# The final norm of all tokens beside the last expert's block, whose own tokens are normed and stored over it

## The chip, the cores and the metric

The kernel runs on one core of a Trainium2 chip. The metric is device time in microseconds of one execution, as the median over several. Engines are named as in the profile: PE (TensorE), PEld (its weight loads), DVE (VectorE), ACT (ScalarE), POOL (GpSimd), SP (SyncE); a q behind a name means the sequencer of that engine.

## What is computed

A layer of a streaming encoder: a mixer (convolution and state space), then a mixture of experts over 2048 tokens of 1024 values, then a final RMS norm. Only the last two matter here.

```python
# top-1 of 4 groups, then top-2 of its 8 experts: 2 of 32 experts per token
h = rms_norm(x, g_ffn[l])
# per expert, in blocks of 128 tokens:
hid = jax.nn.silu(xblk @ w_gate[e]) * (xblk @ w_up[e])
yb = hid @ w_down[e]
x = x + segment_sum(yb * slot_gate, slot_token)      # each token gets two of these rows
return rms_norm(x, g_final)    # x * rsqrt(mean(x*x) + eps) * g_final
```

## The kernel before

`experts()` (L1773) is one block of code for all engines. Each expert has at least one block of 128 slots; the router's counts are known only at run time, so every engine loops in `over_blocks` (L1814): over the 32 experts, and in each over its `n` blocks. At the head of each expert an engine loads `n` and `start` from the tile `counts` into registers (L1817, L1818); ACT and DVE load a third number, `last` (L1819), which equals `n` except for the last expert, where it is never reached. In these inputs there are 46 blocks; the last expert has one.

A block `b`: PE computes gate and up halves (`hidden`), transposes the product (`turn_hidden`) and the next block's x (`turn_x`), and projects down (`down`, L2048). All products are made of float32 split in a high and a low part. DVE's `join` (L1956) makes `hid`, its `hid_low` (L1961) the low part `hl`, `turn_x` (L1950) that of x. ACT scales the result with the gate out of PSUM into `y` (L1906). POOL gathers the tokens of block b+2 (L1849), loads ids and gates (`ids_s`, L1873) as soon as the scatter of the block before has landed, and adds `y` to the rows of `residual` with an accumulating indirect DMA (L1879). Only one such scatter is under way at a time.

Weights: 6 pieces of 1 MB per expert (G0, U0, G1, U1, D0, D1). SP loads them to `raw` (L1629) when the piece before is split. In the last block of each expert but the last, ACT (`split_hi`, L1633) and DVE (`split_lo`, L1637) split those of the next expert between their other work; the test for it is `j == last - 1` (L1916, L2005). The order on DVE there: `join` 0, G0, U0, `hid_low` 0, `join` 1, `turn_x`, `hid_low` 1, G1, U1, D0, D1.

Behind this block of code stands a barrier of all engines (its drains carry line L1781), then `final_norm` (L2092), a block of its own. SP loads the 16 tiles of `residual` in five DMAs (L2109), ACT squares and sums each tile (L2122), DVE makes the scale of each group of tiles in 12 small steps (L2131, L61 to L71) and multiplies each tile by scale and gain (L2136); SP stores each tile when it is made (L2114). All 16 tiles have room in SBUF at once. The end is when all 16 stores have landed.

Of the kernel before, what the change touches and what calls it, by code (L numbers as in the profile page):

```python
# [6 lines left out]
FP32 = mybir.dt.float32  # L7
# [18 lines left out]
T8 = 8  # L26
# [118 lines left out]
def hybrid_encoder(nc, x, w_in, conv_b, log_dt, ssm_d,  # L145
# [21 lines left out]
    with ExitStack() as ctx:  # L167
# [19 lines left out]
        with ExitStack() as moe:  # L187
            weights = ExpertWeights(nc, moe, w_experts)
            experts(nc, scratch, ident, routing, weights)
        final_norm(nc, scratch, g_final, out)  # L190
# [1458 lines left out]
class Routing:  # L1649
# [6 lines left out]
    def __init__(self, nc, ctx):  # L1656
# [7 lines left out]
        self.counts, self.rows = sb("counts", [P, 3, NE], INT32), sb("rows", [1, P], INT32)  # L1664
# [108 lines left out]
def experts(nc, scratch, ident, routing, weights):  # L1773
# [7 lines left out]
    with ExitStack() as ctx:  # L1781
# [6 lines left out]
        y = sb("y", [P, D])  # L1788
        H = F // 2
# [33 lines left out]
        @block.sync  # L1823
        def _(sp):
# [5 lines left out]
            with sp.Fori(1, NE - 1) as e:  # L1830
                for u in range(weights.PIECES):
                    sp.wait_ge(w_lo, e * weights.PIECES + (u + 1))
                    weights.load(sp, e + 1, u)

        @block.gpsimd
        def _(pool):
# [30 lines left out]
            def body(b, e, j, last):  # L1867
# [8 lines left out]
                pool.wait_ge(ids_s_in, b * 16 + 16)  # L1876
                pool.wait_ge(y_done, b * 2 + 2)
# [5 lines left out]
            blocks = pool.value_load(counts[0:1, 1, NE - 1:NE], min_val=0, max_val=NBLK)  # L1883
            blocks = blocks + pool.value_load(counts[0:1, 0, NE - 1:NE], min_val=1, max_val=SEQ // P)
# [4 lines left out]
        def _(act):  # L1889
# [25 lines left out]
            def body(b, e, j, last):  # L1915
                with act.If(j == last - 1):  # L1916
# [24 lines left out]
            over_blocks(act, body, flags=True)  # L1941

        @block.vector
        def _(dve):
# [49 lines left out]
            step(V.tensor_scalar(n[:, NE - 1:NE], n[:, NE - 1:NE], float(2 * NBLK), None, ALU.add))  # L1994
            step(V.tensor_copy(counts[:, 2, :], n))
# [8 lines left out]
            def body(b, e, j, last):  # L2004
                with dve.If(j == last - 1):  # L2005
# [15 lines left out]
            over_blocks(dve, body, flags=True)  # L2021

        @block.tensor
        def _(pe):
# [44 lines left out]
            def body(b, e, j, last):  # L2069
# [9 lines left out]
                wait(pe, y_done, b * 2)  # L2079
# [7 lines left out]
                for i in range(2):  # L2087
                    down(b, 1, i).then_inc(down_done, 1)
            over_blocks(pe, body)


def final_norm(nc, scratch, g_final, out):  # L2092

    GROUPS = ((0, 2), (2, 6), (6, 10), (10, 14), (14, 16))
    with ExitStack() as ctx:  # L2095
        sb, _, sem = alloc(nc, ctx, "final")
        x = sb("x", [P, TT, D])
        gain, junk, st, scale = sb("gain", [P, D]), sb("junk", [P, D]), sb("st", [P, 4, TT]), sb("scale", [P, TT])
        gain_in, squared, own, made, stored = (sem(n) for n in ("gain_in", "squared", "own", "made", "stored"))
        x_in = [sem(f"x_in{g}") for g in range(len(GROUPS))]  # L2100
        block = ctx.enter_context(nc.Block())

        rows = scratch["acc"][0:SEQ, :].rearrange("(i p) d -> p i d", p=P)
        outs = out.rearrange("(h k s) d -> s h k d", s=T8, h=2)

        @block.sync
        def _(sp):
            for g, (first, end) in enumerate(GROUPS):
# [73 lines left out]
```

## Time and profile before

| | us |
|---|---|
| median of 3 runs | 1891.77 |
| lowest and highest run | 1879.50, 1892.37 |
| the profiled execution | 1895.12 |
| its span in the trace | 1893.7 |
| PE busy in the span | 1640.9 |
| DVE busy | 1116.7 |
| ACT busy | 803.3 |
| POOL busy | 605.9 |

Times of rows are microseconds from the start of the span. The profiled execution is 3.35 us longer than the median, and 1.4 us of it lie outside the span. PE's clock was granted at 0.924 of full speed over the span.

### The profile page before, as it was taken

How to read it: one execution, taken by the hardware profiler on the slowest of the kernel's cores; microseconds unless marked ns; L12 is line 12 of the kernel's file. 1: busy time of each engine (PE TensorE's matmuls, PEld its weight loads, DVE VectorE, ACT ScalarE, POOL GpSimd, SP SyncE). 2: the span in 40 equal slices, each digit the busy share in tenths (PEclk: the TensorE clock that was granted, in tenths of full speed). 3: DMA queues.
4: the chain of work that ended last, by engine and by line, in shares of the span. 5: the costliest groups of instructions: out<-in, count | busy, mean ns of one | idle time of the engine just before them, and what ended most of it. 6: DMA issues, size and time to landing. Idle time of an engine off the chain costs nothing. (4 is left out here: it accounts for less than half of the span.)

```text
span 1893.7 us, 33245 instructions
## 1 busy us (share of the span) xinstructions
PE 1640.9 (87%) x11171; PEld 1500.2 (79%) x11172; DVE 1116.7 (59%) x1707; ACT 803.3 (42%) x1022; POOL 605.9 (32%) x882
## 2 busy tenths in 40 slices
PE   7699999688937999999269999999999999999970
PEld 7599999577827888888268999899999888989860
DVE  7845564244547566665617646654666886665546
ACT  3222221012245333342315646644665775665543
POOL 0776774222323336444311212121222121212120
PEclk9899999878968898989579999999999999999995
DMA  8544342498854224312539878885877999887749
GB/s 278 169 146 147 127 161 85 121 223 247 225 200 137 97 89 134 101 67 90 215 119 316 275 240 272 274 285 188 291 273 257 382 366 359 280 275 254 261 137 366
DMA packets 166974, 403.90 MB, mean 213 GB/s; under 512 B 67967, under 2 KB 103169, under 8 KB 140417
## 3 DMA queue, kind: packets, MB, share of 16 engines
q1 hardware_dynamic: 140320, 336.26, 49.7%
q0 software_dynamic: 20080, 58.34, 12.7%
q10 hardware_dynamic: 6512, 8.51, 1.4%
q8 instruction: 36, 0.59, 0.1%
q14 instruction: 26, 0.21, 0.0%
HBM read 313.92 MB, written 89.13 MB: 213 GB/s over the span
## 5 line engine op out<-in xcount | busy, mean ns | idle before, releaser
L1637 DVE TENSOR_TENSOR expert_lo<-expert_raw,expert_hi 128x2048 fp32r<-128x2048 f32 x192 | 430.5, 2284 | 46.4 <-ACT expert_hi L1633 44.6
L1633 ACT CAST expert_hi<-expert_raw 128x2048 fp32r<-128x2048 f32 x192 | 361.6, 1910 | 18.1 <-DMA expert_raw<-in_experts 9.8
L720 PE MATMUL proj_p_z<-proj_x_hi,proj_w_hi 128*128 128x256 f32 x768 | 222.2, 289 | 14.1 <-DVE proj_x_lo L553 14.1
L721 PE MATMUL proj_p_z<-proj_x_lo,proj_w_hi 128*128 128x256 f32 x768 | 218.7, 285 | 0.0
L722 PE MATMUL proj_p_z<-proj_x_hi,proj_w_lo 128*128 128x256 f32 x768 | 218.5, 285 | 0.0
L2037 PE MATMUL moe_p_g0u<-expert_hi,moe_xh 128*128 128x256 f32 x736 | 210.8, 286 | 1.5 <-DVE moe_xl L1950 1.5
L2039 PE MATMUL moe_p_g0u<-expert_lo,moe_xh 128*128 128x256 f32 x736 | 206.6, 281 | 0.0
L2038 PE MATMUL moe_p_g0u<-expert_hi,moe_xl 128*128 128x256 f32 x736 | 206.6, 281 | 0.0
L2052 PE MATMUL moe_p_y<-expert_hi,moe_hh 128*128 128x512 f32 x368 | 153.4, 417 | 13.1 <-DVE moe_hl L1961 13.1
L1879 POOL DMA_INDIRECT residual<-moe_y,moe_ids_s x46 | 78.5, 1708 | 265.6 <-ACT moe_y L1906 258.1
L720 PEld LDWEIGHTS proj_p_z<-proj_x_hi,proj_w_hi 128*128 128x128 f32 x768 | 148.9, 194 | 14.2 <-issue 14.1
L721 PEld LDWEIGHTS proj_p_z<-proj_x_lo,proj_w_hi 128*128 128x128 f32 x768 | 149.0, 194 | 0.1
L722 PEld LDWEIGHTS proj_p_z<-proj_x_hi,proj_w_lo 128*128 128x128 f32 x768 | 148.7, 194 | 0.0
L2053 PE MATMUL moe_p_y<-expert_lo,moe_hh 128*128 128x512 f32 x368 | 145.2, 395 | 0.0
L2037 PEld LDWEIGHTS moe_p_g0u<-expert_hi,moe_xh 128*128 128x128 f32 x736 | 139.6, 190 | 4.0 <-issue 1.9
L2038 PEld LDWEIGHTS moe_p_g0u<-expert_hi,moe_xl 128*128 128x128 f32 x736 | 140.7, 191 | 2.0
L2039 PEld LDWEIGHTS moe_p_g0u<-expert_lo,moe_xh 128*128 128x128 f32 x736 | 139.7, 190 | 0.0
L1956 DVE TENSOR_TENSOR moe_hid<-moe_p_u,moe_sil 128x256 f32<-128x256 f32 x46 | 19.5, 424 | 172.6 <-PE moe_p_u L2039 135.9
L1873 POOL DMA_DIRECT2D moe_ids_s<-slot_table x46 | 25.8, 561 | 283.2 <-DMA residual<-moe_y,moe_ids_s 276.9
L2055 PE MATMUL moe_p_y<-expert_hi,moe_hl 128*128 128x512 f32 x368 | 115.8, 396 | 0.0
L1563 PE MATMUL mix_p_out<-mix_wo_hi,mix_cat_hi 128*128 128x512 f32 x256 | 107.4, 419 | 0.0
L1564 PE MATMUL mix_p_out<-mix_wo_hi,mix_cat_lo 128*128 128x512 f32 x256 | 105.8, 413 | 0.0
(416 smaller groups left out, 4149.9 us busy)
## 6 DMA issues: line engine op xcount, KB each, us to landing
expert_raw<-in_experts SPq DMA_DIRECT2D x192, 1024.0 KB, 6.2
ffn_input<-mix_h SPq DMA_DIRECT2D x17, 512.0 KB, 3.9
proj_x_sb<-in_x SPq DMA_DIRECT2D x8, 1024.0 KB, 7.3
mix_x_sb<-in_x SPq DMA_DIRECT2D x16, 512.0 KB, 5.0
residual<-mix_x SPq DMA_DIRECT2D x16, 512.0 KB, 2.7
out<-final_x SPq DMA_DIRECT2D x16, 512.0 KB, 6.4
proj_x_raw<-in_x_turned SPq DMA_DIRECT2D x7, 1024.0 KB, 4.8
proj_w_raw<-in_w_in SPq DMA_DIRECT2D x8, 768.0 KB, 7.3
```

What stands on the lines that cost most here:

```text
L720: nc.tensor.matmul(o, whi, x_hi[:, half, c], start=start, stop=False)
L721: nc.tensor.matmul(o, whi, x_lo[:, half, c], start=False, stop=False)
L722: return nc.tensor.matmul(o, wlo, x_hi[:, half, c], start=False, stop=stop)
L1563: nc.tensor.matmul(o[:, :], cat_hi[:, par, k, ts], wo_hi[:, k, sl], start=c == 0, stop=False)
L1633: self.nc.scalar.copy(self.hi[:, u], self.raw[:, u]).then_inc(self.hi_done, 1)
L1637: tensor_tensor(self.lo[:, u], self.raw[:, u], self.hi[:, u].bitcast(FP32), ALU.subtract).then_inc(self.lo_done, 1)
L2037: nc.tensor.matmul(out, xh[:, c], w_hi, start=c == 0, stop=False)
L2038: nc.tensor.matmul(out, xl[:, c], w_hi, start=False, stop=False)
L2039: last_mm = nc.tensor.matmul(out, xh[:, c], w_low, start=False, stop=c == KD - 1)
L2052: nc.tensor.matmul(p_y[i][:, :], hh[:, c], w_hi, start=c == 0, stop=False)
L2053: nc.tensor.matmul(p_y[i][:, :], hh[:, c], w_low, start=False, stop=False)
L2055: last_mm = nc.tensor.matmul(p_y[i][:, :], hl[:, c], weights.outer(hi, D0 + i, c), start=False, stop=c == F // P - 1)
```

## The change

The function `final_norm` goes, and with it the barrier ahead of it. `experts()` loops over 31 experts; the last one has code of its own on each engine. When all scatters ahead of the last expert have landed, POOL signals (`acc_complete`), and SP loads the 16 tiles of `residual` in pairs of 1 MB into the six pieces of `raw`, which are free by then. Pair 6 and pair 7 take the room of pairs 0 and 1, once these are stored. ACT squares all tiles (into `y`) and DVE norms them, in groups of 4, 6 and 6 tiles, behind their other work on the last expert's first block. The last expert does not scatter into `residual`: POOL gathers the rows of `residual` of the block's tokens into `r`, DVE adds PSUM times the gate to it, ACT squares it, DVE norms it, and POOL scatters the rows into `out` when all 16 tiles have been stored. `out` has 128 rows more, for the slots that hold no token, and its rows stand in the order of `residual`; the host puts them in order. `counts` loses its third row, and ACT and DVE the value load of `last`.

```diff
-            experts(nc, scratch, ident, routing, weights)
-        final_norm(nc, scratch, g_final, out)
+            experts(nc, scratch, ident, routing, weights, g_final, out)
...
-        self.counts, self.rows = sb("counts", [P, 3, NE], INT32), sb("rows", [1, P], INT32)
+        self.counts, self.rows = sb("counts", [P, 2, NE], INT32), sb("rows", [1, P], INT32)
...
+        gain, r = sb("gain", [P, D]), sb("r", [P, D])
+        fst, fscale, rst = sb("fst", [P, 3, TT]), sb("fscale", [P, TT]), sb("rst", [P, 6])
...
+        LAST = NE - 1
+        PAIRS = TT // 2
+        GROUPS = ((0, 2), (2, 5), (5, 8))
+        gain_in, acc_complete, stored = sem("gain_in"), sem("acc_complete"), sem("stored")
+        tiles_in = [sem(f"tiles_in{g}") for g in range(PAIRS)]
+        squared, norm_own, made = sem("squared"), sem("norm_own"), sem("made")
+        r_in, y_last, r_squared, r_own, r_done = (sem(n) for n in ("r_in", "y_last", "r_squared", "r_own", "r_done"))
...
-        def over_blocks(engine, body, before=None, flags=False):
-            with engine.Fori(0, NE) as e:
+        def tile_of(i):
+            return weights.raw[:, i // 2 % weights.PIECES, i % 2 * D:(i % 2 + 1) * D]
+        def last_blocks(engine):
+            n = engine.value_load(counts[0:1, 0, LAST:NE], min_val=1, max_val=SEQ // P)
+            return n, engine.value_load(counts[0:1, 1, LAST:NE], min_val=0, max_val=NBLK)
+        def over_blocks(engine, body):
+            with engine.Fori(0, LAST) as e:
                 n = engine.value_load(counts[0:1, 0, bass.ds(e, 1)], min_val=1, max_val=SEQ // P)
                 start = engine.value_load(counts[0:1, 1, bass.ds(e, 1)], min_val=0, max_val=NBLK)
-                last = engine.value_load(counts[0:1, 2, bass.ds(e, 1)], min_val=1, max_val=3 * NBLK) if flags else None
                 with engine.Fori(0, n) as j:
-                    body(start + j, e, j, last)
+                    body(start + j, e, j, n)
...
+            acc = scratch["acc"][0:SEQ, :].rearrange("(i p) d -> p i d", p=P)
+            outs = out[0:SEQ, :].rearrange("(i p) d -> i p d", p=P)
+            def load_tiles(g):
+                to = weights.raw[:, g % weights.PIECES].rearrange("p (i d) -> p i d", d=D)
+                sp.dma_start(to, acc[:, 2 * g:2 * g + 2]).then_inc(tiles_in[g], 16)
+            sp.dma_start(gain[:, :], g_final.partition_broadcast(P)).then_inc(gain_in, 16)
+            sp.wait_ge(acc_complete, 1)
+            for g in range(weights.PIECES):
+                sp.wait_ge(w_lo, LAST * weights.PIECES + (g + 1))
+                load_tiles(g)
+            for g in range(PAIRS):
+                for i in (2 * g, 2 * g + 1):
+                    sp.wait_ge(made, i + 1)
+                    sp.dma_start(outs[i], tile_of(i)).then_inc(stored, 16)
+                if g + weights.PIECES < PAIRS:
+                    sp.wait_ge(stored, 32 * (g + 1))
+                    load_tiles(g + weights.PIECES)
+            sp.wait_ge(stored, 16 * TT)
...
-            def body(b, e, j, last):
+            def fetch(b, e, j):
                 pool.wait_ge(x_in, b * 16 + 32)
                 pool.sem_inc(gathers, 1)
                 load_ids(row_of(b + 2))
...
                 pool.wait_ge(x_turned, b * 2 + 4)
                 gather(b + 2)
                 pool.wait_ge(ids_s_in, b * 16 + 16)
+            def body(b, e, j, n):
+                fetch(b, e, j)
                 pool.wait_ge(y_done, b * 2 + 2)
                 pool.sem_inc(scatters, 1)
                 nc.gpsimd.indirect_dma_start(out=scratch["acc"][:, :],
                                              out_offset=bass.IndirectOffsetOnAxis(ap=ids_s[:, 0:1], axis=0),
                                              in_=y[:, :], in_offset=None, compute_op=ALU.add).then_inc(scattered, 16)
             over_blocks(pool, body)
-            blocks = pool.value_load(counts[0:1, 1, NE - 1:NE], min_val=0, max_val=NBLK)
-            blocks = blocks + pool.value_load(counts[0:1, 0, NE - 1:NE], min_val=1, max_val=SEQ // P)
+            n, start = last_blocks(pool)
+            pool.wait_ge(scattered, start * 16 + 16)
+            pool.sem_inc(acc_complete, 1)
+            with pool.Fori(0, n) as j:
+                b = start + j
+                fetch(b, LAST, j)
+                pool.sem_inc(gathers, 1)
+                nc.gpsimd.indirect_dma_start(out=r[:, :], out_offset=None, in_=scratch["acc"][:, :],
+                                             in_offset=bass.IndirectOffsetOnAxis(ap=ids_s[:, 0:1], axis=0)).then_inc(r_in, 16)
+                pool.wait_ge(r_done, j + 1)
+                pool.wait_ge(stored, 16 * TT)
+                pool.sem_inc(scatters, 1)
+                nc.gpsimd.indirect_dma_start(out=out[:, :],
+                                             out_offset=bass.IndirectOffsetOnAxis(ap=ids_s[:, 0:1], axis=0),
+                                             in_=r[:, :], in_offset=None).then_inc(scattered, 16)
+            blocks = start + n
             pool.wait_ge(scattered, blocks * 16 + 16)
             pool.wait_ge(x_in, blocks * 16 + 32)
...
-            def body(b, e, j, last):
-                with act.If(j == last - 1):
+            def squares():
+                for i in range(TT):
+                    act.wait_ge(tiles_in[i // 2], 16)
+                    nc.scalar.activation(y[:, :], tile_of(i), ACT.Square, accum_out=fst[:, 0, i:i + 1]).then_inc(squared, 1)
+                    act.wait_ge(squared, i + 1)
+            def last_expert():
+                n, start = last_blocks(act)
+                with act.Fori(0, n) as j:
+                    b = start + j
+                    silu(b, 0)
+                    silu(b, 1)
+                    hid_high(b, 0)
+                    turn_x(b + 1)
+                    hid_high(b, 1)
+                    with act.If(j == 0):
+                        squares()
+                    for i in range(2):
+                        act.wait_ge(y_last, j * 2 + (i + 3))
+                        nc.scalar.activation(sil[:, :], r[:, i * 512:(i + 1) * 512], ACT.Square,
+                                             accum_out=rst[:, i:i + 1]).then_inc(r_squared, 1)
+                        act.wait_ge(r_squared, j * 2 + (i + 1))
+            def body(b, e, j, n):
+                with act.If(j == n - 1):
...
-            step(V.tensor_scalar(n[:, NE - 1:NE], n[:, NE - 1:NE], float(2 * NBLK), None, ALU.add))
-            step(V.tensor_copy(counts[:, 2, :], n))
...
-                with dve.If(j == last - 1):
+            def final_norm():
+                step = Chain(dve, norm_own)
+                dve.wait_ge(gain_in, 16)
+                for first, end in GROUPS:
+                    dve.wait_ge(squared, 2 * end)
+                    w = slice(2 * first, 2 * end)
+                    step(V.tensor_scalar(fst[:, 1, w], fst[:, 0, w], 0.5 / D, 0.5 * EPS, ALU.mult, ALU.add))
+                    rsqrt(nc, step, fscale[:, w], fst[:, 1, w], fst[:, 2, w])
+                    for i in range(2 * first, 2 * end):
+                        V.scalar_tensor_tensor(out=tile_of(i), in0=tile_of(i), scalar=fscale[:, i:i + 1],
+                                               in1=gain[:, :], op0=ALU.mult, op1=ALU.mult).then_inc(made, 1)
+            def last_expert():
+                n, start = last_blocks(dve)
+                dve.sem_inc(y_last, 2)
+                with dve.Fori(0, n) as j:
+                    b = start + j
+                    join(b, 0)
+                    hid_low(b, 0)
+                    join(b, 1)
+                    turn_x(b + 1)
+                    hid_low(b, 1)
+                    with dve.If(j == 0):
+                        final_norm()
+                    dve.wait_ge(ids_s_in, b * 16 + 16)
+                    dve.wait_ge(r_in, j * 16 + 16)
+                    for i in range(2):
+                        dve.wait_ge(down_done, b * 2 + (i + 1))
+                        half = slice(i * 512, (i + 1) * 512)
+                        V.scalar_tensor_tensor(out=r[:, half], in0=p_y[i][:, :], scalar=ids_s[:, 1:2].bitcast(FP32),
+                                               in1=r[:, half], op0=ALU.mult, op1=ALU.add).then_inc(y_last, 1)
+                    step = Chain(dve, r_own, j * (RSQRT_COLUMN_STEPS + 2))
+                    dve.wait_ge(r_squared, j * 2 + 2)
+                    step(V.tensor_tensor(rst[:, 2:3], rst[:, 0:1], rst[:, 1:2], ALU.add))
+                    step(V.tensor_scalar(rst[:, 3:4], rst[:, 2:3], 0.5 / D, 0.5 * EPS, ALU.mult, ALU.add))
+                    rsqrt_column(nc, step, rst[:, 4:5], rst[:, 3:4], rst[:, 5:6])
+                    assert step.n == RSQRT_COLUMN_STEPS + 2
+                    V.scalar_tensor_tensor(out=r[:, :], in0=r[:, :], scalar=rst[:, 4:5], in1=gain[:, :],
+                                           op0=ALU.mult, op1=ALU.mult).then_inc(r_done, 1)
+            def body(b, e, j, n):
+                with dve.If(j == n - 1):
...
-            over_blocks(dve, body, flags=True)
+            over_blocks(dve, body)
+            last_expert()
...
-            def body(b, e, j, last):
+            def block_of(b, e, room):
                 pe.wait_ge(x_lo, b * 2 + 2)
                 wait(pe, hid_done, b * 2)
...
-                wait(pe, y_done, b * 2)
+                room()
...
+            def body(b, e, j, n):
+                block_of(b, e, lambda: wait(pe, y_done, b * 2))
             over_blocks(pe, body)
...
-def final_norm(nc, scratch, g_final, out):
...
+            n, start = last_blocks(pe)
+            with pe.Fori(0, n) as j:
+                def room():
+                    wait(pe, y_done, start * 2)
+                    pe.wait_ge(y_last, j * 2 + 2)
+                block_of(start + j, LAST, room)
...
-    out = nc.dram_tensor("out", (1, SEQ, D), FP32, kind="ExternalOutput").ap()
+    out = nc.dram_tensor("out", (1, ROWS, D), FP32, kind="ExternalOutput").ap()
     hybrid_encoder(nc, *args, out[0])
     r = _run(nc, [arrays], core_ids=[0])
-    return r.results[0]["out"]
+    by_step = _np.asarray(r.results[0]["out"])[:, :SEQ].reshape(1, T8, 2, P, D)
```

## Rows read from the trace of the kernel before

**Rows 1.** Windows: stretch, its length, busy us (x instructions) of each engine, clock, DMA.
```profile
986.00:1836.00 850.00, 825.47 (x5942) 764.79 (x5940) 540.25 (x456) 510.81 (x547) 174.24 (x180) 1.00 0.82 278
...
1847.00:1894.00 47.00, 0.00 (x0) 0.00 (x0) 29.16 (x76) 18.38 (x32) 0.00 (x0) 0.50 0.93 368
...
1859.00:1871.00 12.00, 0.00 (x0) 0.00 (x0) 6.95 (x17) 9.87 (x17) 0.00 (x0) 0.50 1.03 411
```

**Rows 2.** The page's chain that ended last, by line, as shares of the span.
```profile
DVE final_x L2136 1%; DMA final_x<-residual 1%; ACT final_junk L2122 0%; DVE final_scale L71 0%; DVE final_st L70 0%; DVE final_st L69 0%; DVEq L2095 0%; DVE final_scale L62 0%; DVE final_scale L61 0%; SPq L2111 0%; DVE final_st L2131 0%; SPq L2109 0%; ACTq L2120 0%
```

**Rows 3.** Waits, 1000 to 1836: us in total, times, longest.
```profile
PEld moe_p_hid L2045 <- DVE moe_hid L1956: 15.9, 25, 1.1
...
PE moe_p_y L2052 <- DVE moe_hl L1961: 13.1, 18, 0.8
...
DVE moe_hid L1956 <- issue: 35.1, 30, 1.7
```

**Rows 4.** Timeline of DVE at an expert's begin: start, us, what [idle before].
```profile
1800.17 4.49 DVE L1637 TENSOR_TENSOR expert_lo<-expert_raw,expert_hi 128x2048 fp32r<-128x2048 f32 x2 [1.48 <-ACT expert_hi L1633]
1806.10 0.42 DVE L1956 TENSOR_TENSOR moe_hid<-moe_p_u,moe_sil 128x256 f32<-128x256 f32 x1 [1.44 <-issue]
```

**Rows 5.** DVE sequencer's value loads: whole run, then there: ns min/median/max, starts.
```profile
L1817 DVEq TENSOR_LOAD <-routing_counts x32: 302/844/1387, 964.7 to 1822.6; - x32
...
L1818 DVEq TENSOR_LOAD <-routing_counts x1: 303/303/303, 1804.4 to 1804.4; - x1
...
L1819 DVEq TENSOR_LOAD <-routing_counts x1: 302/302/302, 1805.1 to 1805.1; - x1
```

**Rows 6.** Timeline of ACT: the second half of `y`, last three blocks.
```profile
1797.65 0.69 ACT L1906 ACTIVATE moe_y<-moe_p_y,moe_ids_s 128x512 f32<-128x512 f32 x1 [0.65 <-PE moe_p_y L2055]
...
1817.51 0.69 ACT L1906 ACTIVATE moe_y<-moe_p_y,moe_ids_s 128x512 f32<-128x512 f32 x1 [0.65 <-PE moe_p_y L2055]
...
1835.54 0.69 ACT L1906 ACTIVATE moe_y<-moe_p_y,moe_ids_s 128x512 f32<-128x512 f32 x1 [0.65 <-PE moe_p_y L2055]
```

**Rows 7.** DMA, us to landing: weights; all of tile `final_x`; last scatter.
```profile
expert_raw<-in_experts SPq DMA_DIRECT2D x178, 1024.0 KB, 6.1
...
DMA to landing us min/median/max: 2.7/6.5/22.5
...
residual<-moe_y,moe_ids_s POOLq DMA_INDIRECT x1, 6.3
```

**Rows 8.** Timeline of DVE in the final norm: first small step, first multiplications.
```profile
1854.67 0.17 DVE L2131 TENSOR_SCALAR final_st<-final_st 128x2 f32<-128x2 f32 x1 [22.49 <-ACT final_junk L2122]
...
1857.04 2.48 DVE L2136 SCALAR_TENSOR_TENSOR final_x<-final_x,final_scale,final_gain 128x1024 f32<-128x1024 f32 x2
```

**Rows 9.** Timeline of POOL in the last block.
```profile
1829.63 0.56 POOL L1873 DMA_DIRECT2D moe_ids_s<-slot_table  x1 [5.17 <-DMA residual<-moe_y,moe_ids_s]
...
1837.04 1.66 POOL L1879 DMA_INDIRECT residual<-moe_y,moe_ids_s  x1 [5.45 <-ACT moe_y L1906]
```

**Rows 10.** Timelines of SP and ACT: first load, first and third tile squared.
```profile
1847.44 0.38 SPq L2109 DMA_DIRECT2D final_x<-residual  x1
...
1852.31 1.06 ACT L2122 ACTIVATE final_junk<-final_x 128x1024 f32<-128x1024 f32 x1 [16.08 <-DMA final_x<-residual]
...
1853.49 1.06 ACT L2122 ACTIVATE final_junk<-final_x 128x1024 f32<-128x1024 f32 x1
...
1859.44 1.06 ACT L2122 ACTIVATE final_junk<-final_x 128x1024 f32<-128x1024 f32 x1 [4.80 <-DMA final_x<-residual]
```

**Rows 11.** Timeline of DVE: two subtractions of 128x512 out of PSUM.
```profile
1829.90 1.29 DVE L1950 TENSOR_TENSOR moe_xl<-moe_p_x,moe_xh 128x512 fp32r<-128x512 f32 x2 [0.56 <-ACT moe_xh L1893]
```

**Rows 12.** POOL's drains at the ends of the expert and norm stages: ns, start.
```profile
L1781 POOLq DRAIN  x1: 3615/3615/3615, 1843.6 to 1843.6; - x1
...
L2095 POOLq DRAIN  x1: 46/46/46, 1847.4 to 1847.4; - x1
```

**Rows 13.** The page's DMA queues: the busier instruction queue, whole span.
```profile
q8 instruction: 36, 0.59, 0.1%
```

More of the change, by code:

```diff
@@ L1770, in gates, with experts @@
         step(E.tensor_tensor(pay[:, :, 1, 1].bitcast(FP32), recip, exps[:, :, NG], ALU.mult))
-def experts(nc, scratch, ident, routing, weights):
+def experts(nc, scratch, ident, routing, weights, g_final, out):
     hi, lo, w_lo = weights.hi, weights.lo, weights.lo_done
@@ L1940, in body @@
                         scale_y(b, i)
-            over_blocks(act, body, flags=True)
+            over_blocks(act, body)
+            last_expert()
         @block.vector
@@ L2020, in body @@
                     hid_low(b, 1)
-            over_blocks(dve, body, flags=True)
+            over_blocks(dve, body)
+            last_expert()
         @block.tensor
@@ L2067, in _ @@
             pe.wait_ge(routed, COUNTED)
-            def body(b, e, j, last):
+            def block_of(b, e, room):
                 pe.wait_ge(x_lo, b * 2 + 2)
@@ L2088, in body @@
                     down(b, 1, i).then_inc(down_done, 1)
+            def body(b, e, j, n):
+                block_of(b, e, lambda: wait(pe, y_done, b * 2))
             over_blocks(pe, body)
-def final_norm(nc, scratch, g_final, out):
[L2094 to L2108, printed above, removed]
-                sp.dma_start(x[:, first:end], rows[:, first:end]).then_inc(x_in[g], 16)
-                if g == 0:
-                    sp.dma_start(gain[:, :], g_final.partition_broadcast(P)).then_inc(gain_in, 16)
-            for i in range(TT):
-                sp.wait_ge(made, i + 1)
-                sp.dma_start(outs[i // 2][i % 2], x[:, i]).then_inc(stored, 16)
-            sp.wait_ge(stored, 16 * TT)
-        @block.scalar
-        def _(act):
-            for g, (first, end) in enumerate(GROUPS):
-                act.wait_ge(x_in[g], 16)
-                for i in range(first, end):
-                    nc.scalar.activation(junk[:, :], x[:, i], ACT.Square, accum_out=st[:, 0, i:i + 1]).then_inc(squared, 1)
-                    act.wait_ge(squared, i + 1)
-        @block.vector
-        def _(dve):
-            step = Chain(dve, own)
-            for g, (first, end) in enumerate(GROUPS):
-                dve.wait_ge(squared, end)
-                w = slice(first, end)
-                step(nc.vector.tensor_scalar(st[:, 1, w], st[:, 0, w], 0.5 / D, 0.5 * EPS, ALU.mult, ALU.add))
-                rsqrt(nc, step, scale[:, w], st[:, 1, w], st[:, 2, w])
-                if g == 0:
-                    dve.wait_ge(gain_in, 16)
-                for i in range(first, end):
-                    nc.vector.scalar_tensor_tensor(out=x[:, i], in0=x[:, i], scalar=scale[:, i:i + 1],
-                                                   in1=gain[:, :], op0=ALU.mult, op1=ALU.mult).then_inc(made, 1)
@@ L2177 @@
             for name, a in arrays.items()]
-    out = nc.dram_tensor("out", (1, SEQ, D), FP32, kind="ExternalOutput").ap()
+    out = nc.dram_tensor("out", (1, ROWS, D), FP32, kind="ExternalOutput").ap()
     hybrid_encoder(nc, *args, out[0])
     r = _run(nc, [arrays], core_ids=[0])
-    return r.results[0]["out"]
+    by_step = _np.asarray(r.results[0]["out"])[:, :SEQ].reshape(1, T8, 2, P, D)
+    return _np.ascontiguousarray(by_step.transpose(0, 2, 3, 1, 4)).reshape(1, SEQ, D)
```

## Prediction

> **What bounds the kernel now.** I read the windows first. The expert stage is 850 of the 1893.7 us of the profiled span and PE is busy in 825 of it; in the last 47 us PE is idle, with DVE busy 29 us and ACT 18, and the 11 us between the two hold only the last scatter and a barrier [rows 1]. The chain of waits that ended last runs through the final norm alone: DVE's multiplication first, then the load of the tiles, ACT's squares, DVE's small steps [rows 2]. So the change works on some 57 us, from the last block's scatter to the end. In steady work DMA is the second bound there: share 1.03 at 411 GB/s [rows 1], and the stage reads and writes 8.4 MB each, 41 us at that rate.
>
> Then I read the waits of the expert stage, because the diff also takes something out of a loop that runs 31 more times. PE hardly waits for anything but DVE: 25 waits of its weight loads for `hid` (15.9 us) and 18 for `hl` at the down projection [rows 3]. DVE, on its side, starts `hid` late with no partner named: 30 times "issue", 35.1 us [rows 3]. A timeline shows it: D0 and D1 of the next expert are split by 1804.66, `join` of the next block starts at 1806.10, 1.44 us later [rows 4]; the splits of G0 and U0 and `hid_low` come behind it. In that hole DVE's sequencer does its value loads one after the other: the second starts at 1804.4, the third at 1805.1 [rows 5]. Such an expert of one block takes 19.86 us (second half of `y` at 1797.65 to 1817.51); the block behind it, which has no splits to wait for, takes 18.03 (to 1835.54) [rows 6].
>
> **The change, part by part.**
>
> *One value load less at each expert, on DVE and ACT.* `last` (L1819) goes; the comparison takes `n`. On DVE its load is 0.30 us and the register work around it comes to about as much: start to start it is 0.7 us [rows 5]. I take 0.65, since the starts are rounded. ACT runs ahead in its queue there (no hole), so nothing for it. Where is 0.65 us on the path? In an expert of one block the path is closed: down projection, ACT scales `y`, splits D0, DVE splits D0 and D1, value loads, `join`, two more splits, `hid_low`, down projection. PE waits in it twice, so its own 18 us don't bind and the full 0.65 us comes off. PE's 18 waits for `hl` count these blocks: 18 x 0.65 = 11.7 us. The loads run 32 times [rows 5], the first before any block, so there are 31 boundaries; the other 13 have no splits behind `join`; PE gains only what it waited for `hid`. Of the 25 such waits at least 7 are theirs, mean 15.9 / 25 = 0.64: I take 4 us. Together 15.7 us. Lower bound 0 (if another wait is right behind in each), upper 31 x 0.7 = 21.7. DMA is the cover to look at: with shorter blocks the 6 weight loads of 1 MB per expert come closer together. They land 6.1 us after issue, a third of a block [rows 7], so I cost this at nothing; if that cover went, the gain would be lost where one-block experts stand side by side, at most the 11.7 us.
>
> *Two DVE steps for `counts[:, 2]`* go, once, 0.4 us by the 0.2 us of a small step [rows 8]; beside PE's transpose. Nothing.
>
> *The final norm begins when the scatter before the last has landed.* POOL now sees this with the id load at 1829.63 [rows 9]; it signals SP, whose first load I put at 1829.3 against 1847.44 [rows 10], 18.1 us sooner. Everything of the last block that PE does (to 1835) is covered by this, for DVE comes back to `p_y` only at 1877. The barrier (with POOL's drain of 3.6 us from 1843.6 [rows 12]) goes from between the stages, but see below.
> Loads: the first 1 MB was squared from 1852.31, 4.9 us after its issue; the next 2.5 MB took 7.1 us more [rows 10]. Pair 0 lands at 1834.2. Pairs follow every 2.6 us. POOL's two gathers (the unused one of x and that of `r`, 0.5 MB each, 2.5 us of DMA time) lie between, so pair 4 is in at 1847.1 and pair 5 at 1849.7. ACT needs 1.18 us per tile (1852.31 to 1853.49) [rows 10], keeps up, and has ten tiles squared at 1849.5. DVE's second group: 2.4 us of small steps (1854.67 to 1857.04), six multiplications at 1.2 [rows 8]: 1859.1.
> Now the ring of 6 pieces of `raw` holds 12 tiles. SP waits for tiles 0 and 1 to be stored; their stores lie behind pair 5 on the queue, 1.3 us each: 1852.3. Pair 6 lands at 1857.2; tiles 2 and 3 lie behind it, 1859.8; only then pair 7, landed 1864.7. Its squares are done at 1867.1, small steps 1869.5, six multiplications 1876.7. The stores of tiles 4 to 15 queue behind pair 7: 12 x 1.25 = 15 us, 1879.7.
> The old kernel has its last store landed at about 1893.3, 0.4 us ahead of its end, so the 18 us have become 14 already: two round trips of a store and a load eat the rest.
>
> *The last block's own tokens.* All on the path behind 1876.7: two additions of 128x512 out of PSUM, like those of `xl` (1.29 us for two) [rows 11]; a half tile's square 0.9 with its wait; ten column steps at 0.2, 2.0; a multiplication, 1.3: `r_done` at 1882.3. By then all tiles are stored. POOL starts 0.8 us later, as it does behind `y` (1835.54 and 0.69 against 1837.04) [rows 6, 9]: 1883.1. The scatter without addition is not in the trace: below, a store of as many bytes by SP takes 2.7 us at its shortest [rows 7] and POOL's instruction 1.66 [rows 9], 4.4; above, the accumulating scatter on a quiet chip, 6.3 [rows 7]. I take 5.2, as it has half the traffic of the latter: 1888.3.
>
> *The end.* In the old kernel SP sees its store land and all is over 0.4 us later: POOL, long idle, drains in 46 ns. Behind its own indirect DMAs the same POOL needs 3615 ns [rows 12]. POOL is now the last engine of the last block of code, so this drain moves to the very end: 0.3 + 3.6, 1892.2. Bounds 0.05 and 3.6; I take 3.6, the row of this same place.
> The tail gives 1893.7 - 1892.2 = 1.5 us.
>
> **Sum.** 15.7 + 1.5 = 17.2 us: span 1876.5. The profiled execution took 1895.12 with a median of 1891.77 over the runs; taken off the median, 1874.6, which I call **1875 us**.
>
> The Trainium skill, "DMA: Bandwidth & Descriptors" (section on the anatomy of one DMA on the software path), gives about 2.0 us plus bytes over 436 GB/s for a DMA. For 0.52 MB an estimate from that page is 3.2 us, half of what the quiet scatter's row shows; with it the sum would be 2 us better.
>
> **Rivals.**
> A. *The value load is hidden anyway*: DVE's join then waits for something else as long. For it: DVE's first load of the three takes from 302 to 1387 ns [rows 5], so something unseen stretches it. Against: the loads run one after the other and `join` follows the last. Time: 1891.8 - 1.5 = 1890.
> B. *The tail does worse*: pair 7 comes later, because a load or store under traffic takes 6.5 us in the median [rows 7] and not 1.3 behind a load. Two round trips 4 us longer: tail 8 us worse, 1883.
> C. *Both do better*: a drain of 0.1 us and a scatter of 4.4 make the tail 5.8 us, the loop gives 20: 1891.8 - 25.8 = 1866. For it: no row shows a drain long behind a plain scatter.
> D. *Slower*: code. The last expert has code of its own on every engine, and loops whose code moved may have to be fetched anew at each branch back. It decides from (18.9 + 17.2) / 31 = 1.2 us per expert on PE or DVE; at 1.3 us it gives 1915. Against it: the busier instruction queue carried 36 packets in the whole span [rows 13], against 46 blocks on four engines, so loop bodies stay in place. New straight code for one block falls under the 41 us of slack that PE has.
> Of this the Trainium skill says, in "Runtime: NRT & Kernel Launch", section on instruction fetch, that a taken branch whose target is outside the window of two pages stalls for a fetch. By the packet counts the trace doesn't show that happening in these loops.
>
> **How the numbers follow.** Forecast 0.56 (1868 to 1881, loop 12 to 19 and tail -1 to +5), A 0.17, B 0.10, C 0.11, D 0.06. A measurement of this kernel tells 1% from no change, which is 18.9 us: below 1872.9 is faster, above 1910.7 slower. Of the forecast's own range nearly half lies below 1872.9, with C and a little of the others: faster 0.38; slower D and a rest, 0.07; within 1%, 0.55. The range is 1864 to 1890: it takes in C, B and most of A, leaves out D and the far ends.
>
> **What would show it.** Right: one-block experts of 19.2 us in place of 19.86; DVE's idle "issue" before `hid` near 0.5 us in place of 1.2 (35.1 / 30); PE's waits for `hid` nearly gone; first tile load 18 us ahead of where the old one would be; a hole in ACT's squares before tiles 12 and 14; POOL's scatter last, then a long POOL drain. Wrong: one-block experts still at 19.9 (A), tile 14 squared more than 40 us after the first load (B), a POOL drain under 1 us (C), or holes on PE at each expert with nothing named (D).

## The result and the profile after

| | before | after |
|---|---|---|
| median, us | 1885.63 (4 runs, 1878.65 to 1892.37) | 1861.03 (4 runs, 1853.94 to 1867.52) |
| ratio | | 0.987, 95% interval 0.984 to 0.990 |
| span of the profiled execution, us | 1893.7 | 1865.5 |
| expert stage in the profile, us: from the second half of `y` of block 0 to that of block 44 | 831.07 | 811.18 |
| from there to the end of the span (the tail), us | 76.2 | 76.7 |

The change makes the kernel 1.3% faster. That is outside "within 1%", and 1861.03 is 3 us under the range. The last two rows are the finding in short. They split the span at the second half of `y` of the last block ahead of the last expert (1817.51 in [rows 6]). In the profile of after these are the rows of the timeline of ACT:

```profile
977.61 0.69 ACT L1961 ACTIVATE moe_y<-moe_p_y,moe_ids_s 128x512 f32<-128x512 f32 x1 [0.65 <-PE moe_p_y L2175]
...
1788.79 0.69 ACT L1961 ACTIVATE moe_y<-moe_p_y,moe_ids_s 128x512 f32<-128x512 f32 x1 [0.65 <-PE moe_p_y L2175]
```

The first in the profile of before is:

```profile
986.44 0.69 ACT L1906 ACTIVATE moe_y<-moe_p_y,moe_ids_s 128x512 f32<-128x512 f32 x1 [0.65 <-PE moe_p_y L2055]
```

So 19.9 us of the 28.1 between the two profiles lie in a stage from which the diff takes one value load per expert. 8.8 us lie ahead of block 0, where next to nothing was changed (and the profiled execution of before, 1895.12 us, was slower than all four of the table). In the eleven profiles of this case the stretch ahead of block 0 takes from 971.8 to 986.4 us, whatever the edit. And the stage that was rewritten got 0.6 us longer.

**The loop.** The waits of the expert stage after, in the columns of [rows 3] (us in total, times, longest), answer to those rows:

```profile
PEld moe_p_hid L2165 <- DVE moe_hid L2036: 2.2, 7, 0.4
...
PE moe_p_y L2172 <- DVE moe_hl L2041: 9.1, 16, 0.8
...
DVE moe_hid L2036 <- issue: 13.0, 21, 0.9
```

DVE's hole "issue" before `hid` went from 35.1 to 13.0 us, and PE's waits for `hid` from 15.9 to 2.2. At 9 of the 30 experts that begin between block 0 and block 44 the hole is gone (under 0.1 us), as in this timeline of DVE (start, us, what), to be read against [rows 4]: D0 and D1 are split by 1556.05 and `hid` follows at once. The next expert's `hid` comes 18.40 us later; for the same expert it was 19.10 before (1579.62 to 1598.72, the last two lines).

```profile
1551.56 4.49 DVE L1636 TENSOR_TENSOR expert_lo<-expert_raw,expert_hi 128x2048 fp32r<-128x2048 f32 x2 [1.49 <-ACT expert_hi L1632]
1555.97 0.42 DVE L2036 TENSOR_TENSOR moe_hid<-moe_p_u,moe_sil 128x256 f32<-128x256 f32 x1
...
1574.37 0.42 DVE L2036 TENSOR_TENSOR moe_hid<-moe_p_u,moe_sil 128x256 f32<-128x256 f32 x1
```
```profile
1579.62 0.42 DVE L1956 TENSOR_TENSOR moe_hid<-moe_p_u,moe_sil 128x256 f32<-128x256 f32 x1 [1.02 <-issue]
...
1598.72 0.42 DVE L1956 TENSOR_TENSOR moe_hid<-moe_p_u,moe_sil 128x256 f32<-128x256 f32 x1 [0.69 <-issue]
```

Where the loads lie explains the hole. Here are DVE's two value loads at the expert above, then at one where a hole was left (its last split ends at 1776.55, `hid` starts at 1777.40):

```profile
L1835 DVEq TENSOR_LOAD <-routing_counts x1: 347/347/347, 1554.1 to 1554.1; - x1
...
L1836 DVEq TENSOR_LOAD <-routing_counts x1: 324/324/324, 1554.8 to 1554.8; - x1
```
```profile
L1835 DVEq TENSOR_LOAD <-routing_counts x1: 1323/1323/1323, 1774.6 to 1774.6; - x1
...
L1836 DVEq TENSOR_LOAD <-routing_counts x1: 319/319/319, 1776.3 to 1776.3; - x1
```

At each of the 30 beginnings, in all eleven profiles, the first load starts 1.92 to 1.96 us ahead of the end of the last split, and where a hole is left `hid` starts 0.73 or 0.85 us behind the end of the last load (0.93 or 1.05 in e9, which has arithmetic there). So the first 1.1 to 1.2 us of the loads are hidden under the last split; only what goes beyond that is the hole. In the kernel before every hole was at least 0.67 us long, so the third load, 0.30 us and 0.41 us of register work behind the second, came off almost in full.

**The tail.** SP's timeline, then ACT's and DVE's (the part on the path), then POOL's last scatter and, from the view of one line, its drain:

```profile
1800.08 3.11 SPq L1857 DMA_DIRECT2D expert_raw<-residual  x6
1814.25 1.55 SPq L1867 DMA_DIRECT2D out<-expert_raw  x2
1823.78 0.38 SPq L1857 DMA_DIRECT2D expert_raw<-residual  x1
...
1832.95 0.38 SPq L1857 DMA_DIRECT2D expert_raw<-residual  x1
```
```profile
1830.52 1.06 ACT L1974 ACTIVATE moe_y<-expert_raw 128x1024 f32<-128x1024 f32 x1 [6.82 <-DMA expert_raw<-residual]
...
1839.23 1.06 ACT L1974 ACTIVATE moe_y<-expert_raw 128x1024 f32<-128x1024 f32 x1 [6.38 <-DMA expert_raw<-residual]
```
```profile
1841.59 0.17 DVE L2089 TENSOR_SCALAR moe_fst<-moe_fst 128x6 f32<-128x6 f32 x1 [10.76 <-ACT moe_y L1974]
...
1844.01 7.26 DVE L2092 SCALAR_TENSOR_TENSOR expert_raw<-expert_raw,moe_fscale,moe_gain 128x1024 f32<-128x1024 f32 x6
...
1855.82 1.28 DVE L2120 SCALAR_TENSOR_TENSOR moe_r<-moe_r,moe_rst,moe_gain 128x1024 f32<-128x1024 f32 x1
```
```profile
1858.00 0.98 POOL L1936 DMA_INDIRECT out<-moe_r,moe_ids_s  x1 [47.84 <-DVE moe_r L2120]
```
```profile
L1782 POOLq DRAIN  x1: 3697/3697/3697, 1861.6 to 1861.6; - x1
```

The first load starts 11.3 us behind the `y` of block 44; in the old kernel [rows 10] it was 29.9 us. The 18.6 us won there are spent again, in two places. From the first load to the end of the last multiplication the new kernel takes 51.2 us (1800.08 to 1851.27), the old one 43.1 (1847.44 to 1890.54, the end of the line below): ACT stands 6.8 us and then 6.4 us for pairs 6 and 7, whose loads SP may issue only at 1823.78 and 1832.95, when tiles 0 and 1, then 2 and 3, are stored; DVE stands 10.8 us. Behind the last tile come 6.7 us of the last block's own tokens, 3.3 us of scatter and 3.7 us of drain, 14.3 us with what lies between; the old kernel had its own tokens, its scatter and that drain ahead of its norm, and 3.1 us behind it. So 8.1 and 11.1 us more, 19.2 together.

```profile
1888.06 2.48 DVE L2136 SCALAR_TENSOR_TENSOR final_x<-final_x,final_scale,final_gain 128x1024 f32<-128x1024 f32 x2
```

### The profile page after: what moved, and what is told of

It reads as the page before. It is cut to its first block, busy times and chain, and to the rows that moved or that the text cites. A ratio compares the mean times of both kernels' runs of the same rounds, so it can differ in the third digit from the quotient of the medians.

```text
span 1865.5 us, 32975 instructions
## 1 busy us (share of the span) xinstructions
PE 1628.9 (87%) x11171; PEld 1493.3 (80%) x11172; DVE 1116.0 (60%) x1694; ACT 801.1 (43%) x1024; POOL 603.0 (32%) x883
## 4 chain that ended last, share of the span: by engine, by line
PE 33%; issue 6%; DMA 4%; DVE 3%; ACT 2%; DVEq 2%; POOL 1%; ACTq 0%; SPq 0%; POOLq 0%
PE moe_p_y L2172 5%; PE moe_p_y L2175 4%; PE moe_p_y L2173 4%; PE moe_p_g0u L2157 3%; PE moe_p_g0u L2159 3%; PE moe_p_g0u L2158 3%; DVE expert_lo L1636 2%; ACT expert_hi L1632 2%; PE moe_p_x L2149 1%; PE moe_p_g L2159 1%; PE moe_p_u L2159 1%; PE moe_p_g L2158 1%; PE moe_p_u L2157 1%; PE moe_p_u L2158 1%; PE moe_p_g L2157 1%
## 5 line engine op out<-in xcount | busy, mean ns | idle before, releaser
L1920 POOL DMA_INDIRECT residual<-moe_y,moe_ids_s x45 | 76.5, 1700 | 251.8 <-ACT moe_y L1961 244.3
```

## Experiments

Each median below stands beside runs of the kernel before on the same chip. The length of the expert stage is always the time from the second half of `y` of block 0 to that of block 44, from a kernel's profile.

**e1: the loop alone.** The kernel before with its final norm and barrier kept, and the load of `last` gone from ACT and DVE. These two engines loop over 31 experts and have the last one's block behind the loop (not shown in the cut).

```diff
-            with engine.Fori(0, NE) as e:
+            with engine.Fori(0, NE - 1 if flags else NE) as e:
...
-                last = engine.value_load(counts[0:1, 2, bass.ds(e, 1)], min_val=1, max_val=3 * NBLK) if flags else None
                 with engine.Fori(0, n) as j:
-                    body(start + j, e, j, last)
+                    body(start + j, e, j, n)
...
```

> The kernel before, with its final norm and barrier as they were; only the third value load of ACT and DVE at each expert is gone (both loop over 31 experts, the last has code of its own on these two engines). Theory: the load on DVE's sequencer is nearly the whole gain, since in the two profiles the expert stage shrank by 19.9 us from the end of block 0 to the end of block 44 and the tail behind it by -0.5. So 19 to 21 us below before, ratio 0.989. Rival (the gain is that of the overlapped final norm): 0 to 3 us below before, ratio 0.999.

Measured: 1867.35 us against 1884.79, ratio 0.990 (0.988 to 0.992). The stage takes 811.01 us:

```profile
980.33 0.69 ACT L1909 ACTIVATE moe_y<-moe_p_y,moe_ids_s 128x512 f32<-128x512 f32 x1 [0.65 <-PE moe_p_y L2077]
...
1791.34 0.69 ACT L1909 ACTIVATE moe_y<-moe_p_y,moe_ids_s 128x512 f32<-128x512 f32 x1 [0.65 <-PE moe_p_y L2077]
```

With the old norm and barrier and no overlap at all, the same 20 us of the stage are there. The medians lie 17.4 us apart, somewhat less than the 19 to 21 expected; the interval, 14.5 to 23.0 us, takes in both.

**e2: the new tail with the old number of loads.**

```diff
                 start = engine.value_load(counts[0:1, 1, bass.ds(e, 1)], min_val=0, max_val=NBLK)
+                last = engine.value_load(counts[0:1, 0, bass.ds(e, 1)], min_val=1, max_val=SEQ // P) if third else n
                 with engine.Fori(0, n) as j:
-                    body(start + j, e, j, n)
+                    body(start + j, e, j, last)
```

> The kernel after with a third value load put back on ACT and DVE at each of the 31 experts (it loads n again). Theory: the expert stage is back at 831 us from block 0 to 44, and the time is within 2 us of before if the 5 us that the medians show beyond the expert stage are chance, or 5 us below before if something else in the change gives them. Rival (overlap is the gain): it stays at 1861, 24 us below before.

Measured: 1884.51 against 1884.79, ratio 1.000 (0.998 to 1.002). The stage is back at 829.3 us, the tail is 76.5:

```profile
974.53 0.69 ACT L1962 ACTIVATE moe_y<-moe_p_y,moe_ids_s 128x512 f32<-128x512 f32 x1 [0.65 <-PE moe_p_y L2176]
...
1803.87 0.69 ACT L1962 ACTIVATE moe_y<-moe_p_y,moe_ids_s 128x512 f32<-128x512 f32 x1 [0.65 <-PE moe_p_y L2176]
```

The overlap of the final norm with the last expert is worth nothing as it stands. The rival that it carries the gain falls. PE's waits for `hid` are back too:

```profile
PEld moe_p_hid L2166 <- DVE moe_hid L2037: 19.2, 25, 1.6
```

**e3: the third load on ACT only.** As e2, with `third=True` for ACT alone.

> The kernel after with the third value load put back on ACT alone. Theory: ACT's sequencer does it while ACT still works on the splits, so it costs nothing: 23 to 25 us below before, as after. Rival (either engine's loads count, the loop is as tight on ACT): 10 us or more given back.

Measured: 1866.20 against 1884.79, ratio 0.989 (0.987 to 0.992); stage 808.3 us. The load costs nothing on ACT; with e2 this leaves DVE's as the one that counts. By the medians the kernel is 18.6 us below before and not 23 to 25 as expected: that figure rested on the median of after, of which more under e4.

**e4: the order of the output rows.** The kernel before with `out` as in the change (contiguous tiles, 128 rows more).

> The kernel before with only the output changed: 128 rows more, and its rows in the order of the residual, so each tile is stored to one contiguous stretch. Theory that the 5 us outside the expert stage are chance: same as before, within 1 us. Rival (memory layout or the order of the stored rows is worth something): 3 to 6 us below before.

Measured: 1889.92 against 1884.79, ratio 1.002 (1.000 to 1.004); stage 832.4 us, tail 76.2. The gain of 3 to 6 us of the rival isn't there. "Within 1 us" was missed as well: the medians lie 5.1 us the other way, though stage and tail in the profile are within 1.4 us of those of before. So what the medians of after show beyond the stage (24.6 against 19 to 20 us) has no cause in the output. e1 and e3, with the same loop, come 17.4 and 18.6 us below before. That the rest is spread is likely: 23 runs of before beside e1 to e4 lie between 1869.77 and 1896.13, differences of 5 us turn up in both directions (e4), and the interval of the ratio of after, 0.984 to 0.990, means 19 to 30 us and takes in the 19.3 us that the parts give. That is argued, not shown.

**e5: room for all tiles.** Pairs 6 and 7 get 16 KB per partition of their own.

```diff
+        extra = sb("extra", [P, 2, 2 * D])
...
+            for g in range(weights.PIECES, PAIRS):
+                load_tiles(g)
+            for i in range(TT):
+                sp.wait_ge(made, i + 1)
+                sp.dma_start(outs[i], tile_of(i)).then_inc(stored, 16)
```

> The kernel after, but pairs 6 and 7 of the tiles have room of their own (16 KB per partition more), so SP issues all eight loads at once and waits for no store. Theory: the two round trips of store and load took the tail's gain. In the profile of after pair 5 landed 21 us and pair 7 39 us behind the first load's issue; pair 7 should land near 27, the last multiplication come 10 us sooner and the end 10 to 11 us sooner: tail 66 us in place of 76.7, about 1.6% below before. Rival (DMA as such is the bound, and the waits only hide it): the stores end as late as now and the tail gains under 3 us.

Measured: 1859.05 against 1883.55, ratio 0.986 (0.983 to 0.990). In the profile the tail is 65.5 us, 11.3 shorter, as expected. SP issues all loads at once, and DMA runs mostly at 400 to 430 GB/s from then until the last tile's store (SP's timeline, the DMA view's GB/s in 40 slices of 1809 to 1864, and POOL's timeline):

```profile
1809.67 3.39 SPq L1860 DMA_DIRECT2D expert_raw<-residual  x6
1813.10 4.16 SPq L1860 DMA_DIRECT2D moe_extra<-residual  x2
```
```profile
GB/s 0 113 402 399 334 329 411 426 423 420 417 417 411 426 423 420 411 420 426 426 417 417 414 420 426 417 420 417 417 429 417 420 414 77 0 164 218 0 0 0
```
```profile
1856.41 0.99 POOL L1937 DMA_INDIRECT out<-moe_r,moe_ids_s  x1 [36.37 <-DMA out<-moe_extra]
```

So the two round trips cost 11.3 of the 19.2 us that the tail had lost; the part behind the last tile stays. What bounds the tail now is DMA and DVE together: pair 4 lands at 1827.8, DVE then works without a hole from 1830.2 to 1849.5, and the last store, issued there behind others, lands 6.0 us later and lets POOL go. The medians show none of the 11 us (24.5 us below before, after 24.6). In this profile the stage took 814.4 us, the longest of the kernels with two loads, and the stretch ahead of block 0 took 984.1, 6.5 more than in that of after; 5 runs don't settle 10 us at such a spread.

**e6: the last block's own tokens in DVE's hole.** On DVE `final_norm(GROUPS[:2])` ahead of them and `GROUPS[2:]` behind, and likewise on ACT.

> The kernel after with the last block's own tokens normed on DVE between the second and third group of tiles, in the hole in which DVE waits for the squares of the last tiles (10.8 us in the profile of after), and on ACT between tiles 11 and 12. Theory: the 6.7 us from the last tile's multiplication to POOL's scatter leave the path; POOL then waits for the last stores, which land 3 us behind that multiplication, so the tail is 3 to 4 us shorter: 73 us. Rival (the end is set by stores and scatter, not by this work): no change.

Measured: 1860.49 against 1883.55, ratio 0.987 (0.982 to 0.991); tail 73.5 us, 3.2 shorter. That is as expected in the profile, and too small for the medians. POOL now waits for the stores:

```profile
1848.49 0.98 POOL L1936 DMA_INDIRECT out<-moe_r,moe_ids_s  x1 [45.01 <-DMA out<-expert_raw]
```

**e8: no last scatter.** The kernel leaves out the last expert's part of its tokens.

```diff
-                pool.sem_inc(scatters, 1)
-                nc.gpsimd.indirect_dma_start(out=out[:, :],
...
-            pool.wait_ge(scattered, blocks * 16 + 16)
+            pool.wait_ge(scattered, start * 16 + 16)
```

> The kernel after without POOL's last scatter: the rows of the last expert's tokens stay as the final norm of all tokens left them, without that expert's part. It shows what POOL's drain at the end hangs on. Theory (a fixed price of a POOL that has issued indirect DMAs in this block of code, whatever was last): the drain still takes 3.6 to 3.7 us though its last DMA was issued 48 us before, and the tail is 3.4 to 4.3 us shorter, the scatter alone. Rival (the drain waits for what the scatter just issued): the drain is below 0.2 us and the tail 7 us shorter.

Measured, a single execution: 1858.57 us, tail 72.4 us, 4.4 shorter. The drain is there all the same, with POOL's last DMA (the gather of `r`, issued at 1805.23) 48 us back:

```profile
1805.23 0.97 POOL L1931 DMA_INDIRECT moe_r<-residual,moe_ids_s  x1 [0.30 <-issue]
```
```profile
L1782 POOLq DRAIN  x1: 3612/3612/3612, 1853.3 to 1853.3; - x1
```

So it isn't a price of the last scatter. POOL's drains at the ends of two earlier blocks of code point the same way. The one ahead of the expert stage, below from the kernel before, starts when POOL's engine has been idle for 2.6 us; the block had 24 indirect DMAs. At 315.2 us one behind 16 DMAs took 1.38 us. The expert stage issues 197 DMAs on POOL and its drain takes 3.6 us; the norm of the kernel before issues none, 0.05 us. So the length seems to go with what POOL issued in the block; what exactly it clears, the trace doesn't tell.

```profile
L1054 POOLq DRAIN  x1: 2194/2194/2194, 908.8 to 908.8; - x1
```

**e9: one load in place of two.** On top of e5, for DVE alone:

```diff
+                if packed:
+                    both_in = engine.value_load(counts[0:1, 2, bass.ds(e, 1)], min_val=1, max_val=64 * NBLK + 63)
+                    start = both_in // 64
+                    n = both_in - start * 64
```

> As e5_more_room, and DVE loads one number per expert, start times 64 plus n, and takes it apart with register arithmetic, in place of two value loads. Theory: DVE's sequencer still sets the start of hid by 0.5 us on average at each of the 30 boundaries (mean idle 0.49 us at one-block experts, 0.35 at the others in the profile of after), so if the arithmetic costs less than a load with its bounds (0.7 us), 5 to 10 us more come off the expert stage. Rival (the first load's own varying time, 0.3 to 1.4 us, sets it, or the division costs as much as the load): within 2 us of e5.

Measured: 1849.41 against 1883.55, ratio 0.981 (0.978 to 0.984), the best here. The stage takes 803.5 us (e5 814.4, after 811.2), the tail 66.1. The rival, within 2 us of e5, falls. Of DVE's holes 2.8 us are left between 985 and 1778, where after has the 13.0 us in the same stretch:

```profile
DVE moe_hid L2044 <- issue: 2.8, 10, 0.4
```

**e10: four loads on DVE.** Two more `value_load` of `n` ahead of the inner loop.

> The kernel after with two value loads more on DVE alone, four at each expert. Theory (in a one-block expert the path through DVE is closed, so each load adds its full length; at the others as soon as PE waits): the first load put back cost 0.6 to 0.7 us at each of 30 boundaries; the fourth adds 0.7 to 0.8 at all of them, so from the end of block 0 to the end of block 44 it takes 850 to 856 us (after 811, before 831), and one-block experts take 20.4 to 20.6 us. Rival (something else of the load row or of the loop's code made the difference, and a load itself is cheap): 831 us or less.

Measured, a single execution: 1904.02 beside one of before, 1900.81, on another chip than the runs above; two such times say little. The stage in the profile takes 844.0 us:

```profile
981.56 0.69 ACT L1964 ACTIVATE moe_y<-moe_p_y,moe_ids_s 128x512 f32<-128x512 f32 x1 [0.65 <-PE moe_p_y L2178]
...
1825.59 0.69 ACT L1964 ACTIVATE moe_y<-moe_p_y,moe_ids_s 128x512 f32<-128x512 f32 x1 [0.65 <-PE moe_p_y L2178]
```
```profile
PEld moe_p_hid L2168 <- DVE moe_hid L2039: 36.7, 30, 1.7
```

Longer, as the theory asks, but 6 us under its lower bound, and one-block experts take 20.2 us on average where it asked for 20.4 to 20.6. The theory priced a load at 0.7 to 0.8 us; these two take 0.62 us each, start to start (0.30 us and 0.32 of register work). The kernels with 1, 2, 3 and 4 loads that share the code of after stand side by side here (e9 has the tail of e5). The hole is DVE's idle time before the first `hid` of the 30 experts, the wait is that of PE's weight loads for `hid`:

| loads on DVE | kernel | stage, us | hole in total, us | PE's waits, us |
|---|---|---|---|---|
| 1 | e9 | 803.5 | 3.1 | 0 |
| 2 | after | 811.2 | 13.1 | 2.2 |
| 3 | e2 | 829.3 | 32.9 | 19.2 |
| 4 | e10 | 844.0 | 51.8 | 36.7 |

The hole grows by 10, 20 and 19 us. The first step is small because the loads fit under the last split in 18 of 30 cases with one load, in 9 with two, and in none with three. The last is 30 times 0.62 us. The stage grows by less, 8, 18 and 15 us; why the last step gives 4 us less than its hole was not found. The kernel before, whose third load has 0.41 us of register work and not 0.32, takes 831.1 us.

One thing more varies. The first of the loads takes anything from 0.3 to 1.4 us on DVE (mean over 30 boundaries between 0.73 and 0.91 us in these profiles) and about 0.3 on every other engine. A difference of 0.1 us in that mean is 3 us of the hole, so this alone can shift the stage by some us between kernels with the same loads: six profiles with two loads lie between 808.3 and 814.4, three with three between 829.3 and 832.4. What stretches the first load was not found.

## Why the prediction was right and wrong

The finding that the value load matters and the overlap hardly does was right. Of the two parts, the loop gained as forecast, and more; the tail, forecast to gain 1.5 us, lost 0.6. The time left the range below, through these terms:

| | predicted, us | measured, us |
|---|---|---|
| base (median of before) | 1891.77 | 1885.63 |
| expert stage | -15.7 | -19.9 (e1 by its profile -20.1) |
| tail | -1.5 | +0.6 |
| rest, in no part that was changed | 0 | -5.3 |
| after | 1875 | 1861.03 |

The step that failed is the one from the effects to the time: "taken off the median, 1874.6". The effects were forecast at 17.2 us and the parts measure 19.3, so they account for 2.1 of the 14 us; the base, a median of three, and the rest, which looks like spread too, account for 11.4. That the effects come within 2.1 is partly luck: the loop was forecast 4.2 us too low and the tail 2.1 too well.

1. **The base.** That step took a median of three runs from 1879.5 to 1892.37 as if it were known to a microsecond. Over the 23 runs beside e1 to e4, before has a median of 1884.79. That alone is 6 to 7 of the 14 us. The range was laid around the sum of effects and held nothing for the base. The rest of 5.3 us lies in neither changed part; the profiles place such differences ahead of block 0 (971.8 to 986.4 us), and the ratio's interval covers it.
2. **The value load, 0.65 us each** and 15.7 us in all. The mechanism and the place were right (e1, e2, e3), the term was too small. The 18 one-block experts took 19.70 us on average before and 18.91 after, from the last weight load of one block to that of the next: 0.79 each and 14.3 in all, where 11.7 were predicted. The other boundaries gave 4.6 (4 predicted) and blocks that begin no expert 0.9 (nothing predicted). DVE's hole at one-block experts fell from 1.29 to 0.49 us, so 0.80 left it. Of this 0.71 is the load with its register work, below which the prediction chose 0.65; the rest goes with the varying first load, whose mean over all beginnings was 0.86 us in the profile of before and 0.77 in that of after; it moves as much between kernels with the same loads. The upper bound of 21.7 held. One reading was off without harm: the loads don't begin in the hole but 1.94 us ahead of the split's end. Had the holes been shorter than a load, its price would not have come off in full, as in e9.
3. **Rival A** (hidden anyway) fell with e1. Its ground, the varying first load, is real, but it comes on top of the others and doesn't cover them.
4. **The tail: pairs 6 and 7.** The two round trips were there. The step that failed in the tail is the landing of pairs 6 and 7 at 4.9 us, as for the first load on a quiet queue: with stores behind them they took 6.7 and 6.2 us. From the first load's start, pair 7 landed after 39.1 us where 35.4 stand in the prediction. That is the mechanism of rival B at half its size; e5 shows the place by taking the round trips away, 11.3 us.
5. **The last block's own tokens** took 6.7 us from the last tile to POOL's start (5.6 and 0.8 predicted). **The scatter** landed after 3.3 us, below the lower bound of 4.4; that bound had 1.66 us for POOL's instruction, which took 0.98. The estimate from the Trainium skill, "DMA: Bandwidth & Descriptors", section on the anatomy of one DMA on the software path, was 3.2 us, and this trace agrees.
6. **The drain** moved to the very end at 3.7 us, as predicted, and e8 shows in one execution that it doesn't hang on the last scatter. Rival C's drain of 0.1 us is out.
7. **Rival D** (code fetched anew in the loops). The busier instruction queue carried 37 packets after and 36 before [rows 13], and PE's holes without a name between 1000 and 1789 come to 0.3 us in the profile of after.
8. **DMA in the one-block experts** was costed at nothing and cost nothing: there the block took 18.4 us (1555.97 to 1574.37), and between block 0 and block 44 no engine waited for a weight load, though such a load landed 8.0 us after its issue in the median, 6.2 before.
9. **The chances.** "Within 1%" had 0.55 and "faster" 0.38. By the parts (19.3 us, 1.02%) the case lies on the line; e1, the loop alone, came out at 0.990. Which side of the line the medians fall on is not settled by the parts.

## What to carry to other kernels

A register load at the head of a dynamic loop is on the path when its engine is the one that closes the loop. Count its sequencer's start-to-start times, 0.6 to 0.7 us here, less what is hidden under the engine's last instruction, and multiply by the trips before looking at the big parts of a change. Overlapping a stage with the one ahead of it pays only if it gets the room to run through and leaves nothing behind itself: of 18.6 us won at the start, six buffers for eight transfers cost 11.3 in two round trips, and the last block's own work and the drain had moved to the end. And before a range is drawn around a sum of effects, look at how far the base's own runs lie apart.

## What had not been expected of the hardware

- A value load from SBUF takes 302 to 1387 ns on DVE's sequencer when it is the first at an expert, the next ones 0.3 us in the median and up to 0.6 (kernel before); on PE's, ACT's and POOL's sequencers it takes 0.3 us in the median and at most 0.5 at the same place.
- DVE's first value load starts 0.33 to 0.37 us into the last split ahead of it, at each of 30 beginnings in eleven profiles, so that what is left of the split hides part of the loads.
- A plain indirect scatter of 128 rows of 4 KB landed after 3.3 us, the accumulating one of the same bytes after 6.3 us on a quiet chip [rows 7].
- POOL's drain at the end of a block of code took 3.6 us also when its last DMA lay 48 us back (e8), and 2.2 and 1.4 us at the ends of earlier blocks with fewer DMAs.
